# A decoder-layer step: the sample loop runs in four turns of two samples and two prompt heads instead of eight turns of one

## The chip, the cores and the metric

The kernel is one program on one core of a Trainium2 chip. TensorE (PE) multiplies matrices, VectorE (DVE), ScalarE (ACT) and GpSimd (POOL) work on vectors, SyncE (SP) issues transfers. The metric is the device time in microseconds (us), the median of several runs.

## What is computed

One inference step of one layer, in float32, for a prompt of 256 rows and for 8 samples of one row each, each sample with 2048 past rows of K and V in 16 pages. The width is 1024, attention has 8 heads of 64, the depthwise convolution 512 channels and 31 taps, and the feed-forward part 2816 inner channels.

```python
h = rms_norm(x, g_norm1) * (1.0 + sc1) + sh1
q, k, v, glu_a, glu_b, gate_a, gate_c = split(h @ w_in)        # q, k are normed per head
attn = moba_attention(q, k_all, v_all, pos0, slopes) @ w_attn_proj
u = glu_a * sigmoid(glu_b)
cv = depthwise_causal_conv(concat(conv_past, u), w_dwconv) + b_dwconv
cv = silu(layer_norm(cv)) @ w_conv_proj
mix = (sigmoid(gate_a) * attn + sigmoid(gate_c) * cv) @ w_out
x = x + gt1 * mix
h2 = rms_norm(x, g_norm2) * (1.0 + sc2) + sh2
x = x + gt2 * ((silu(f_g) * f_u) @ w_ffn_out)                  # f_g, f_u = halves of h2 @ w_ffn_in
```

`moba_attention` lets each query see its own block of 256 rows and the three past blocks whose mean key fits it best. The outputs are the rows of both groups, their new K and V rows, and the last rows of the convolution's input. sh, sc and gt are parts of `silu(c) @ w_ada + b_ada`.

## The kernel before, in words

All 264 rows (256 prompt, 8 samples) lie transposed, channels on the partitions. Each engine has its own list of instructions in an order written by hand, and semaphores tie the lists together; an engine whose next instruction waits does nothing else meanwhile.

**Prelude.** Modulation, norm, and the columns of q, k, v and the first two pairs of GLU columns (a0, b0, a1, b1). These are made as three products of high and low parts (`split`, L1459).

**The sample loop**, `for b in range(B)`, eight turns. Turn b finishes sample b and prompt head b, and does meanwhile the scoring of sample b + 1 on VectorE. The scoring of one sample is four steps, each a multiplication of four pages of K with the sample's query (`multiply`, L1053, 128x2048) and a reduction over the head's 64 channels (`add_up`, L1060). Both work on one buffer `prod`, so each waits for the one before. K comes in 16 chunks of half a sample by indirect DMA from POOL's queue, into a ring of three places, V in 16 such chunks into a ring of two. The small instructions of a turn lie between these halves:

- the sample: block sums by PE (L1621), their copy (L1156, the first instruction of a turn on VectorE), the gates of the blocks, a ranking of the 8 blocks and penalties (L1168 to L1186), the mask (L1650), maximum (L1198, L1205), exp on ACT, sum (L1220), weights `pg` (L1232); then PE's product with V (`weigh_values`, L1607), the turn of its result (`turn_values`, L1614)
- the head: scores by PE (`prompt_scores`), ALiBi (L1165), maxima (L1170, L1173), exp and scaling on ACT, transposes (L1675), product with V (L1690)
- on PE, to fill gaps, the gate columns g0 to g15 and the rest of the GLU columns (a2, b2, a3, b3), three in a turn (`tile`, L1455); ACT evacuates them with Sigmoid
- on ACT and POOL the 120 taps of the convolution, 20 in each of six turns: a scaled copy (ACT) and an addition (POOL, L575).

The layer norm over the convolution's channels is done in turns 6 and 7. The last turn has no scoring and no gate column.

**After the loop** come the UNITS: eight columns of the convolution's projection (`conv_unit`, cp0 to cp7), eight of attention's (ap0 to ap7), eight of w_out, 44 and then 8 of the feed-forward part (the last in three pieces each). Each unit's weights are split by ACT and VectorE into high and low parts (`whi`, `wlo`), at most four units ahead. Before unit 0, `weigh_values(7)` is issued. Between the units stand the remaining modulations, by ADA_AFTER: modulation(4) behind unit 3, modulation(5) behind unit 9, modulation(6) behind unit 13.

**SyncE** issues the loads of weights one after another in the order of SLOTS, each when its place is free. The order around the change is the gate slots mix0 to mix6, then conv, attn, mod4, out0, mod5, out... as

```python
         + ["conv", "attn", "mod4", "out0", "mod5", "mod6", "out1", "mod7", "mod8", "mod9"]
```

mod5 takes the place of mod4 once modulation(4) has read it. out0 lies in the memory that V's ring had, and for it SyncE has

```python
                if name == "out0":
                    sp.wait_ge(v_used, CH * B)
```

where v_used counts the two halves of each `weigh_values`, 16 in all.

Of the kernel before, what the change touches and what calls it, by code (L numbers as in the profile page):

```python
# [48 lines left out]
THIRD = {0: "a2", 1: "b2", 2: "a3", 3: "b3", 4: "g10", 5: "g13"}  # L49
FIRST_GATE = (0, 2, 4, 6, 8, 11, 14)  # L50


SLOTS = (["ada0", "ada1", "ada2", "ada3", "q", "k", "v", "glu"] + [f"mix{n}" for n in range(B - 1)]
# [17 lines left out]
ADA_AFTER = {3: 4, 9: 5, 13: 6, FIRST_OUT + 1: 7, FIRST_OUT + 3: 8, FIRST_OUT + 5: 9}  # L71
ADT_AFTER = {5: 4, 11: 5, 15: 6, FIRST_OUT + 2: 7, FIRST_OUT + 4: 8, FIRST_OUT + 6: 9, FIRST_FFN + 5: 10, FIRST_FFN + 9: 11}
# [3 lines left out]
PLACE = dict(zip(SLOTS, [0, 1, 2, 0, 1, 2, 0, 1] + [n % 2 for n in range(B - 1)]))  # L76
# [7 lines left out]
         + [f"{x}{t}" for x in "qkv" for t in range(4)] + ["a0", "b0", "vn0", "vn1", "vs", "ks", "kn0", "kn1", "so", "a1", "b1"])  # L84
for _b in range(B - 1):
    FILLS.append(f"g{FIRST_GATE[_b]}")
    if _b == B - 2:
        FILLS += ["ct", "lnm"]
    FILLS.append(f"g{FIRST_GATE[_b] + 1}")
    FILLS.append(THIRD.get(_b, "lnv"))  # L90
# [19 lines left out]
for _b in range(B - 1):  # L110
    LAST_FILL[f"mix{_b}"] = THIRD.get(_b, f"g{FIRST_GATE[_b] + 1}")

# [3 lines left out]
CONV_LOOPS = 6  # L116
CONV_PART = CT * (TAPS - 1) // CONV_LOOPS
CONV_SPLIT = (6, 6, 8)


def program(nc, x_prompt, x_sample, cache_k, cache_v, state_conv, page_table, c_prompt, c_sample,
# [3 lines left out]
    with ExitStack() as ctx:  # L125
# [9 lines left out]
        def sem(name):  # L135
# [20 lines left out]
        inquad = sb("inquad", [P, QU, P], F32R)  # L156
# [11 lines left out]
        sall = sb("sall", [P, 2, PG, H])  # L168
        s1 = sb("s1", [P, PG + 1, H])
        sown = sb("sown", [P, B, H])  # L170
        pg = sb("pg", [P, PG, H])
# [4 lines left out]
        gsT = sb("gsT", [P, QU])  # L176
        gate = sb("gate", [H, NB])
        lanes = pvm[:, 0:P]
        cmp1, cmp2 = (mrow[0:H, 0, 64 * e:64 * e + 64].rearrange("p (m n) -> p m n", m=NB) for e in range(2))
        pen = sb("pen", [H, NB, H], F32R)  # L180
        spots = pvm[:, P:2 * P]
        powns = gs[:, :, 0:H]
        tiny = sb("tiny", [P, 64])
        m1, nmx, dg, es, rinv, pown = (tiny[:, 0:8], tiny[0:H, 8:9], tiny[0:H, 16:24], tiny[:, 24:32],
                                       tiny[:, 32:40], tiny[32:32 + B, 40:48])
        bars = tiny[0:H, 56:64]
        pmx, psum_, prin = tiny[:, 48:50], tiny[:, 50:52], tiny[:, 52:54]
# [40 lines left out]
        vrow = vT[32:32 + B, :, :].rearrange("p t r -> p (t r)")[:, 0:A]  # L228
        snat = u[0:B, 2:4, TAPS - 1:TAPS - 1 + A // 2]
# [12 lines left out]
        soq = s1[0:B, 0:2 * B, :].rearrange("p g h -> p (g h)").rearrange("p (t n) -> p t n", t=2)  # L242
        headsums = oT[0:2 * H, 0, :]
        samples = pg[:, :, :].rearrange("p g h -> p (g h)")
# [22 lines left out]
        modrow_bank, modcol_bank = psS[:, 0:P], chain[:, 0:P]  # L267
        spread_factor = small[:, 0:R]
        normbank = [psS, psT, chain, small, psS, psT]
        sums_, gate_, mask_, turned_ = small[:, 0:QU], small[0:H, 8:8 + NB], small[:, 0:P], small[0:H, P:2 * P]  # L270
        spread_max, spread_sum = small[:, 0:H], small[:, 16:16 + H]
# [44 lines left out]
        ln_c, ln_s, cv_ready = sem("ln_c"), sem("ln_s"), sem("cv_ready")  # L316
# [60 lines left out]
        def conv_part(b, part):  # L377

            if b >= CONV_LOOPS:
                return range(0)  # L380
            first = CONV_PART * b + sum(CONV_SPLIT[:part])
            return range(first, first + CONV_SPLIT[part])


        @block.sync
        def _(sp):
            def load(name):
# [5 lines left out]
                if name == "mod4":  # L393
                    sp.wait_ge(v_full[CH - 1], 16 * B)
# [31 lines left out]
                elif kind == "mix":  # L426
                    wide = P * (3 if THIRD.get(num, "")[:1] == "g" else 2)
                    parts = [(full[:, :, 0:wide], cols(w_in, glu0 + 2 * C + P * FIRST_GATE[num], wide))]
                    if num < 4:
                        parts.append((full[:, :, 2 * P:3 * P], cols(w_in, glu0 + C * (num % 2) + P * (num // 2 + 2), P)))  # L430
# [36 lines left out]
        def _(pool):  # L467
# [57 lines left out]
            step(g.memset(inquad[:, :, :].bitcast(F32), 0.0))  # L525
            for q in range(QU):
                step(g.memset(inquad[0:H, q, 32 * q:32 * q + 32].bitcast(F32), 1.0))
# [40 lines left out]
            def add_taps(b, part):  # L568

                for i in conv_part(b, part):  # L570
                    t = i // (TAPS - 1)
                    pool.wait_ge(prod_ready, i + 1)
                    if i >= 1:
                        pool.wait_ge(conv_added, i)
                    g.tensor_tensor(cvT[:, t, 0:S], cvT[:, t, 0:S], cprod[:, i % CONV_RING, :], ALU.add)\  # L575
                        .then_inc(conv_added, 1)
# [11 lines left out]
            for name in ON_POOL:  # L588
# [3 lines left out]
                if name == "k0":  # L592
                    gather_k(1)
                if name == "v0":
                    pool.wait_ge(acc_full, NUMBER[LAST_FILL["k"]] + 1)
                    gather_k(2)
                if name == "v2":
                    gather_k(3)
                if name == "v3":
                    gather_v(0, 0)  # L600
                if name == "b1":
                    gather_k(4)
            for b in range(B):
# [4 lines left out]
                else:  # L608
                    for c in range(CH):
                        gather_v(b, c)  # L610
# [314 lines left out]
        def _(dve):  # L925
# [210 lines left out]
            for b in range(B):  # L1136
# [86 lines left out]
                if b == 6:  # L1223
                    center()
# [558 lines left out]
```

## Time and profile before

| what | value |
|---|---|
| median of 3 runs | 582.43 us (580.84 to 582.52) |
| the profiled execution's own time | 581.04 us |
| its span, first to last instruction | 579.3 us |
| mean granted TensorE clock | 0.953 of full speed |
| busy: PE, DVE, ACT, POOL | 521.1, 395.7, 292.4, 170.2 us |
| read and written in HBM | 159.1 MB, 275 GB/s over the span |

Busy time is an average over stages with different limits, so the rows below are taken from single stretches. Times in rows are microseconds from the start of the span, unless ns is written. One PE matmul on float32 shows as two instructions, and its end is modelled: where it counts, PE's pace is read from start to start.

### The profile page before, as it was taken

How to read it: one execution, taken by the hardware profiler on the slowest of the kernel's cores; microseconds unless marked ns; L12 is line 12 of the kernel's file. 1: busy time of each engine (PE TensorE's matmuls, PEld its weight loads, DVE VectorE, ACT ScalarE, POOL GpSimd, SP SyncE). 2: the span in 40 equal slices, each digit the busy share in tenths (PEclk: the TensorE clock that was granted, in tenths of full speed). 3: DMA queues.
4: the chain of work that ended last, by engine and by line, in shares of the span. 5: the costliest groups of instructions: out<-in, count | busy, mean ns of one | idle time of the engine just before them, and what ended most of it. 6: DMA issues, size and time to landing. Idle time of an engine off the chain costs nothing.

```text
span 579.3 us, 10395 instructions
## 1 busy us (share of the span) xinstructions
PE 521.1 (90%) x4166; PEld 440.6 (76%) x4166; DVE 395.7 (68%) x609; ACT 292.4 (50%) x519; POOL 170.2 (29%) x232
## 2 busy tenths in 40 slices
PE   3769899888989889798879999599999999999997
PEld 3558688764565557456539999499999999999996
DVE  0643683789999799999766886758565656555441
ACT  3234434587777677755474542383444444433431
POOL 8416378288777586760100000000000000000000
PEclk9589899989989798999969999899999999999999
DMA  8999549698999999999689969937565456476501
GB/s 302 371 359 385 192 164 374 227 351 304 405 411 398 406 345 406 381 402 387 253 328 371 387 244 372 364 129 227 183 216 185 147 176 164 107 200 173 148 18 38
DMA packets 82127, 159.31 MB, mean 275 GB/s; under 512 B 2572, under 2 KB 61112, under 8 KB 76951
## 3 DMA queue, kind: packets, MB, share of 16 engines
q1 hardware_dynamic: 76256, 89.27, 46.1%
q0 software_dynamic: 5120, 67.71, 29.2%
q10 hardware_dynamic: 703, 1.67, 0.8%
q8 instruction: 33, 0.54, 0.4%
q14 instruction: 15, 0.12, 0.1%
HBM read 156.39 MB, written 2.72 MB: 275 GB/s over the span
## 4 chain that ended last, share of the span: by engine, by line
PE 52%; DVE 23%; DMA 12%; issue 5%; ACT 5%; POOL 2%; ACTq 1%; SPq 1%; DVEq 0%; POOLq 0%
PE acc L1583 11%; PE acc L1584 11%; PE acc L1585 11%; DVE prod L1053 7%; DMA wring<-in_w_in 6%; DVE sall L1060 5%; PE acc L1455 4%; DMA wring<-in_w_ffn_in 2%; DVE wlo L1125 2%; PE acc L1468 2%; DMA more<-in_w_ada 2%; PE acc L1470 2%; PE acc L1469 2%; DMA pr<-in_page_table 2%; PE chain L1607 1%
## 5 line engine op out<-in xcount | busy, mean ns | idle before, releaser
L1125 DVE TENSOR_TENSOR wlo<-wring,whi 128x1024 fp32r<-128x1024 f32 (+2 forms) x84 | 92.0, 1097 | 70.9 <-ACT whi L620 69.9
L620 ACT ACTIVATE whi<-wring 128x1024 fp32r<-128x1024 f32 (+2 forms) x84 | 80.0, 958 | 81.3 <-PE acc L1585 74.4
L1583 PE MATMUL acc<-xlo,whi 128*128 128x264 f32 x384 | 110.1, 287 | 0.3 <-DVE hT L1332 0.2
L1584 PE MATMUL acc<-xhi,wlo 128*128 128x264 f32 x384 | 108.9, 284 | 0.0
L1585 PE MATMUL acc<-xhi,whi 128*128 128x264 f32 x384 | 108.8, 283 | 0.0
L575 POOL TENSOR_TENSOR cvT<-cvT,cprod 128x256 f32<-128x256 f32 x120 | 88.0, 733 | 43.9 <-ACT cprod L620 29.0
L1455 PE MATMUL acc<-hT,wring 128*128 128x264 f32 x336 | 94.2, 425 | 4.1 <-DMA wring<-in_w_in 3.7
L1455 PEld LDWEIGHTS acc<-hT,wring 128*128 128x128 f32 x336 | 65.3, 206 | 18.8 <-DMA wring<-in_w_in 4.2
L1583 PEld LDWEIGHTS acc<-xlo,whi 128*128 128x128 f32 x384 | 72.3, 188 | 1.4 <-issue 0.6
L1060 DVE TENSOR_REDUCE sall<-prod 128x32 f32<-128x2048 f32 x32 | 73.0, 2281 | 0.4
L1584 PEld LDWEIGHTS acc<-xhi,wlo 128*128 128x128 f32 x384 | 72.4, 188 | 0.0
L1585 PEld LDWEIGHTS acc<-xhi,whi 128*128 128x128 f32 x384 | 72.0, 188 | 0.0
L620 ACT ACTIVATE cprod<-u,vt 128x256 f32<-128x256 f32 x120 | 53.6, 501 | 13.8 <-POOL cvT L575 12.8
L1584 PE MATMUL acc<-fhi,wlo 128*128 128x264 f32 x208 | 59.2, 284 | 0.0
L1585 PE MATMUL acc<-fhi,whi 128*128 128x264 f32 x208 | 58.9, 283 | 0.0
L1053 DVE TENSOR_TENSOR prod<-kring,qbc 128x2048 f32<-128x2048 f32 x22 | 50.0, 2273 | 1.3 <-PE qbc L1485 0.7
L1583 PE MATMUL acc<-flo,whi 128*128 128x264 f32 x176 | 50.0, 284 | 0.3 <-ACT yn L620 0.3
L620 ACT ACT_TABLE_LOAD x36 | 46.2, 1283 | 2.3 <-PEq L1772 1.7
L586 POOL TENSOR_TENSOR wrest<-wring,phi 128x1024 fp32r<-128x1024 f32 x14 | 33.9, 2428 | 38.2 <-ACT phi L620 38.2
L1585 PEld LDWEIGHTS acc<-fhi,whi 128*128 128x128 f32 x208 | 39.1, 188 | 0.0
L1584 PEld LDWEIGHTS acc<-fhi,wlo 128*128 128x128 f32 x208 | 39.1, 188 | 0.0
L1468 PE MATMUL acc<-hsplit,phi 128*128 128x264 f32 x120 | 36.5, 304 | 0.8 <-POOL wrest L586 0.8
(317 smaller groups left out, 907.9 us busy)
## 6 DMA issues: line engine op xcount, KB each, us to landing
wring<-in_w_ffn_in SPq DMA_DIRECT2D x22, 1024.0 KB, 8.0
wring<-in_w_ada SPq DMA_DIRECT2D x20, 1024.0 KB, 11.4
wring<-in_w_in SPq DMA_DIRECT2D x12, 1024.0 KB, 11.4
wring<-in_w_ffn_out SPq DMA_DIRECT2D x16, 704.0 KB, 5.6
more<-in_w_out SPq DMA_DIRECT2D x4, 1024.0 KB, 12.3
more<-in_w_ada SPq DMA_DIRECT2D x4, 1024.0 KB, 12.5
wring<-in_w_in SPq DMA_DIRECT2D x6, 512.0 KB
wring<-in_w_in SPq DMA_DIRECT2D x4, 768.0 KB
```

Of the source, the lines that this page charges most:

```text
L575: g.tensor_tensor(cvT[:, t, 0:S], cvT[:, t, 0:S], cprod[:, i % CONV_RING, :], ALU.add)\
L586: g.tensor_tensor(low, w, high.bitcast(F32), ALU.subtract).then_inc(rest_by_pool, 1)
L620: return nc.scalar.activation(out, in_, f, **kw)
L1053: v.tensor_tensor(prod[:, :, :], k_place[chunk % K_RING][:, g:g + n, :], qbc[b % 2][:, :].unsqueeze(1).to_broadcast([P, n, A]), ALU.mult). ...
L1060: v.tensor_reduce(sall[:, b % 2, n * half:n * half + n, :].rearrange("p g h -> p (g h)"), prod[:, :, :].rearrange("p g (h d) -> p (g h) d" ...
L1125: v.tensor_tensor(wlo[:, place, 0:n, :], w, whi[:, place, 0:n, :].bitcast(F32), ALU.subtract)\
L1455: ins = mm(bank[:, 0:R], w[:, k, P * t:P * t + P], src[:, k, :], start=k == 0, stop=k == KD - 1)
L1468: mm(bank[:, 0:R], high[:, k, :], hlo[:, k, :], start=k == 0, stop=False)
L1469: mm(bank[:, 0:R], low[:, k, :], hhi[:, k, :], start=False, stop=False)
L1583: mm(bank[:, 0:R], whi[:, place, k - k0, :], lo[:, k, :], start=k == 0, stop=False)
L1584: mm(bank[:, 0:R], wlo[:, place, k - k0, :], hi[:, k, :], start=False, stop=False)
L1585: ins = mm(bank[:, 0:R], whi[:, place, k - k0, :], hi[:, k, :], start=False, stop=k == nk - 1)
```

## The change

The loop becomes four turns of a pair of samples and two prompt heads. What a sample needs between its scores and its weights is done for both at once: block sums, ranking, mask, maxima, exp, sum, weights (128 x 2 x 16 x 8 instead of 128 x 16 x 8). The head's work stays per head. Scoring stays a turn ahead, which is now two samples ahead: sample 1 is scored before the loop too, and each of the first three turns scores two samples, eight steps, of which the last three have nothing between their halves. The fourth turn scores nothing, and holds both samples' and both heads' work, the whole layer norm and the four gate columns g12 to g15. `weigh_values(7)` and `turn_values(7)` move from the start of the units to behind conv unit 5 and 6. modulation(5) moves from behind unit 9 to behind unit 7. The wait of mod4's load for V is dropped, that of out0 stays. Gate and GLU columns have five slots of four columns instead of seven of three. POOL issues some gathers of K and V earlier, and takes the taps in parts of five, 40 in each of three turns.

Sigmoid(x) is written as (1 + tanh(x/2)) / 2: ACT does Tanh with scale 0.5, VectorE adds 1 in the product that follows, and the half goes into GLU's copy and into gt1. The layer norm's root is split in a scaling on VectorE and a Sqrt on ACT.

In the order of VectorE's, ACT's and PE's lists (context lines of the loop on VectorE are the old instructions at their new place):

```diff
+PAIRS = B // 2
+TILES = (("a2", "b2", "a3", "b3", "g0", "g1"), tuple(f"g{n}" for n in range(2, 7)),
+         tuple(f"g{n}" for n in range(7, 12)), tuple(f"g{n}" for n in range(12, 16)))
+MIX = [["a2", "a3", "b2", "b3"]] + [[f"g{4 * n + t}" for t in range(4)] for n in range(4)]
+HOME = {name: (f"mix{n}", t) for n, names in enumerate(MIX) for t, name in enumerate(names)}
...
-ADA_AFTER = {3: 4, 9: 5, 13: 6, FIRST_OUT + 1: 7, FIRST_OUT + 3: 8, FIRST_OUT + 5: 9}
-ADT_AFTER = {5: 4, 11: 5, 15: 6, FIRST_OUT + 2: 7, FIRST_OUT + 4: 8, FIRST_OUT + 6: 9, FIRST_FFN + 5: 10, FIRST_FFN + 9: 11}
+ADA_AFTER = {3: 4, 7: 5, 13: 6, FIRST_OUT + 1: 7, FIRST_OUT + 3: 8, FIRST_OUT + 5: 9}
+ADT_AFTER = {5: 4, 10: 5, 15: 6, FIRST_OUT + 2: 7, FIRST_OUT + 4: 8, FIRST_OUT + 6: 9, FIRST_FFN + 5: 10, FIRST_FFN + 9: 11}
...
-                if name == "mod4":
-                    sp.wait_ge(v_full[CH - 1], 16 * B)
                 if name == "out0":
                     sp.wait_ge(v_used, CH * B)
...
+                if name == "k2":
+                    gather_v(0, 0)
...
+            gather_k(5)
+            pool.wait_ge(acc_full, NUMBER["b1"] + 1)
+            gather_v(0, 1)
+            for i in range(PAIRS):
+                gather_k(4 * i + 6)
+                add_taps(i, 0)
+                if i >= 1:
                     for c in range(CH):
-                        gather_v(b, c)
-                add_taps(b, 1)
-                gather_k(CH * b + 5)
-                add_taps(b, 2)
-                gather_k(CH * b + 6)
+                        gather_v(2 * i, c)
+                add_taps(i, 1)
+                gather_k(4 * i + 7)
+                add_taps(i, 2)
+                add_taps(i, 3)
+                gather_k(4 * i + 8)
+                add_taps(i, 4)
+                for c in range(CH):
+                    gather_v(2 * i + 1, c)
+                add_taps(i, 5)
+                gather_k(4 * i + 9)
...
-                    freed(func(cvT[:, t, :], bank[:, 0:R], ACT.Sigmoid), f"b{t}")
+                    freed(func(cvT[:, t, :], bank[:, 0:R], ACT.Tanh, scale=0.5), f"b{t}")
...
+            last, a = PAIRS - 1, B - 2
+            act.wait_ge(k_used, STEPS * B)
+            for n in range(AHEAD):
+                split_weights(n)
+            head_exp(a)
+            column(last, 0)
+            values_copied(a - 1)
+            tails_of_conv()
+            head_scaled(a)
+            column(last, 1)
+            values_out(a - 1)
+            sample_exp(last)
+            head_turned(a)
+            column(last, 2)
+            head_out(a)
+            head_exp(a + 1)
+            column(last, 3)
+            wait_freed(act, "lnv")
+            func(lnf, lnf, ACT.Sqrt).then_inc(ln_v, 1)
+            head_scaled(a + 1)
+            values_copied(a)
+            values_out(a)
+            head_turned(a + 1)
+            head_out(a + 1)
+            conv_rows()
 
             def split_row(t, ready):
...
-                if n_unit >= 2:
-                    split_weights(n_unit + AHEAD)
+                split_weights(n_unit + AHEAD)
                 if n_unit - 1 in ADA_AFTER:
                     mod_rows(ADA_AFTER[n_unit - 1])
-                if n_unit == 5:
+                if n_unit == 6:
+                    values_copied(B - 1)
+                if n_unit == 7:
+                    values_out(B - 1)
                     act.wait_ge(ownt_ready, 2)
...
+            score(1, 1)
+            score(1, 2)
+            own_scores()
+            dve.wait_ge(consts, 3)
+            gated_glu(0)
+            dve.wait_ge(u_ready, 1)
+            score(1, 3)
...
+                multiply_next(0)
+                turned_sums(i)
                 add_up_next(0)
+                if i == 0:
+                    gated_glu(1)
                     wait_freed(dve, "so")
+                head_scores(a)
+                penalties(i)
                 multiply_next(1)
+                masked(i)
                 add_up_next(1)
+                head_inverse(a)
+                diagonal(i)
                 multiply_next(2)
+                below_maximum(i)
+                if i == 0:
+                    gated_glu(2)
                 add_up_next(2)
+                partition_sums(i)
                 multiply_next(3)
+                weights(i)
                 add_up_next(3)
+                if i == 0:
+                    gated_glu(3)
+                multiply_next(4)
+                head_scores(a + 1)
+                add_up_next(4)
+                head_inverse(a + 1)
+                for n in range(5, 2 * STEPS):
+                    multiply_next(n)
+                    add_up_next(n)
+                if i == 0:
                     dve.wait_ge(stored, 16 * 7)
...
+            last, a = PAIRS - 1, B - 2
+            turned_sums(last)
+            head_scores(a)
+            penalties(last)
+            samples_convolution()
+            masked(last)
+            head_inverse(a)
+            diagonal(last)
+            center()
+            below_maximum(last)
+            split_weights(0)
+            partition_sums(last)
+            weights(last)
+            bank = when_full(dve, "lnv")
+            freed(v.tensor_scalar(lnf, bank[:, 0:R], 1.0 / C, EPS, ALU.mult, ALU.add), "lnv")
+            head_scores(a + 1)
+            split_weights(1)
+            head_inverse(a + 1)
+            split_weights(2)
+            dve.wait_ge(ln_v, 1)
+            step(v.reciprocal(lnf, lnf))
+            scale_rows()
+            for t in range(CT):
+                dve.wait_ge(rhi_ready, t + 1)
+                v.tensor_tensor(clo[:, t, :], cvT[:, t, :], chi[:, t, :].bitcast(F32), ALU.subtract)\
+                    .then_inc(rlo_ready, 1)
+            conv_branch(0)
...
+            for i in range(PAIRS - 1):
+                a = 2 * i
+                first = 1 if i == 0 else 0
+                block_sums(i)
+                column(i, 0, k1=5)
+                gates_of_blocks(i)
+                if i >= 1:
+                    weigh_values(a - 1)
+                else:
+                    column(i, 0, k0=5)
+                    column(i, 1, k1=5)
+                mask(i)
+                column(i, first, k0=5)
+                column(i, first + 1, k1=4)
+                turn_maxima(i)
+                if i >= 1:
+                    turn_values(a - 1)
+                spread_query(a + 3)
+                column(i, first + 1, k0=4)
+                spread_maxima(i)
+                turn_head(a, a)
+                column(i, first + 2)
+                total(i)
+                weigh_head(a)
+                prompt_scores(a + 1)
+                column(i, first + 3, k1=6)
+                weigh_values(a)
+                column(i, first + 3, k0=6)
+                turn_values(a)
+                if i < PAIRS - 2:
+                    spread_query(a + 4)
+                column(i, first + 4, k1=4)
+                turn_head(a + 1, a + 1)
+                column(i, first + 4, k0=4)
+                weigh_head(a + 1)
+                prompt_scores(a + 2)
+            last, a = PAIRS - 1, B - 2
+            block_sums(last)
+            column(last, 0)
+            gates_of_blocks(last)
+            weigh_values(a - 1)
+            to_rows("ct", u, S, TAPS - 1 + B)
+            mask(last)
+            pe.wait_ge(ln_c, 1)
+            sums("lnm", cvT, CT)
+            column(last, 1)
+            turn_maxima(last)
+            turn_values(a - 1)
+            spread_maxima(last)
+            turn_head(a, a)
+            pe.wait_ge(ln_c, 2)
+            sums("lnv", lnsq, CT)
+            column(last, 2)
+            total(last)
+            weigh_head(a)
+            prompt_scores(a + 1)
+            column(last, 3)
+            weigh_values(a)
+            turn_values(a)
+            turn_head(a + 1, a + 1)
+            weigh_head(a + 1)
...
-            weigh_values(B - 1)
-            conv_unit(0)
-            conv_unit(1)
-            turn_values(B - 1)
-            for t in range(2, KD):
+            for t in range(KD):
+                if t == 6:
+                    weigh_values(B - 1)
+                if t == 7:
+                    turn_values(B - 1)
                 conv_unit(t)
                 if t == 4:
                     pe.wait_ge(ownrow_ready, 1)
```

The new functions are the old groups under names: `turned_sums` is L1156, `head_scores` L1165, L1170 and L1173, `head_inverse` L1203, `penalties` L1168 to L1186 without the maxima, `masked` L1195 and L1198, `diagonal` L1205 and L1207, `below_maximum` L1214, `partition_sums` L1220, `weights` L1227 to L1234. On PE `column(i, n)` is the n-th column of TILES[i], in part where k0 or k1 is given; `turn_head` and `weigh_head` are L1675 and L1690. In `penalties` each instruction now waits for the one before it, while before the head's maxima lay between them.

## Rows read from the trace of the kernel before

**Rows 1.** The chain that ended last, shares of the span by engine.

```profile
PE 52%; DVE 23%; DMA 12%; issue 5%; ACT 5%; POOL 2%; ACTq 1%; SPq 1%; DVEq 0%; POOLq 0%
```

**Rows 2.** Busy us (instructions) per engine, PE's clock, DMA share, GB/s.

```profile
157.80:182.70 24.90, 22.32 (x120) 14.54 (x116) 24.08 (x32) 18.91 (x40) 18.44 (x25) 0.93 1.03 404
...
234.90:259.30 24.40, 20.87 (x120) 13.56 (x116) 24.00 (x32) 16.93 (x35) 17.39 (x23) 1.00 1.00 399
...
283.50:302.00 18.50, 14.74 (x96) 6.15 (x97) 11.20 (x31) 10.16 (x24) 1.89 (x2) 0.72 0.65 250
```

**Rows 3.** VectorE's timeline, scoring steps: start, duration, instruction.

```profile
64.00 2.29 DVE L1053 TENSOR_TENSOR prod<-kring,qbc 128x2048 f32<-128x2048 f32 x1 [0.71 <-PE qbc L1485]
...
68.71 2.29 DVE L1053 TENSOR_TENSOR prod<-kring,qbc 128x2048 f32<-128x2048 f32 x1
...
230.25 2.29 DVE L1060 TENSOR_REDUCE sall<-prod 128x32 f32<-128x2048 f32 x1
232.67 2.29 DVE L1053 TENSOR_TENSOR prod<-kring,qbc 128x2048 f32<-128x2048 f32 x1
234.87 0.15 DVE L1156 COPY gsT<-small 128x4 f32<-128x4 f32 x1
...
259.28 0.15 DVE L1156 COPY gsT<-small 128x4 f32<-128x4 f32 x1
```

**Rows 4.** VectorE's timeline, small instructions with POOL adding taps, and after.

```profile
237.19 0.60 DVE L1165 SCALAR_TENSOR_TENSOR pr<-distm,slopes,psS 128x384 f32<-128x384 f32 x1
...
238.50 0.61 DVE L1175 SCALAR_TENSOR_TENSOR mrow<-mrow,lower 8x64 f32<-8x64 f32 x1
...
262.90 0.20 DVE L1175 SCALAR_TENSOR_TENSOR mrow<-mrow,lower 8x64 f32<-8x64 f32 x1
```

**Rows 5.** VectorE's timeline, end of the prelude, and the layer norm's centring.

```profile
96.02 0.48 DVE L1042 SCALAR_TENSOR_TENSOR qkvT<-qkvT,vt,psT 128x264 f32<-128x264 f32 x1
104.82 0.16 DVE L1156 COPY gsT<-small 128x4 f32<-128x4 f32 x1 [8.32 <-PE small L1621]
...
275.17 1.26 DVE L1111 TENSOR_TENSOR cvT<-cvT,cprod 128x1056 f32<-128x1056 f32 x1
```

**Rows 6.** PE's timeline: half a gate column, value products, first and last conv unit's edges.

```profile
246.31 2.05 PE L1455 MATMUL acc<-hT,wring 128*128 128x264 f32 x8
...
257.31 3.62 PE L1607 MATMUL chain<-vring,pg 128*8 128x512 f32 x32
...
283.11 0.38 PE L1621 MATMUL small<-quad,sall 128*128 128x4 f32 x2 [0.80 <-DVE sall L1060]
...
296.63 5.08 PE L1607 MATMUL chain<-vring,pg 128*8 128x512 f32 x32
301.65 0.39 PE L1583 MATMUL acc<-clo,whi 128*128 128x264 f32 x1
...
318.59 0.36 PE L1583 MATMUL acc<-fhi,whi 128*128 128x264 f32 x1 [0.74 <-DVE wlo L1125]
```

**Rows 7.** ACT's timeline: a table load before an exp, and the four Silus.

```profile
263.13 1.28 ACT L620 ACT_TABLE_LOAD   x1
264.42 0.40 ACT L620 ACTIVATE pr<-pr,tiny 128x128 f32<-128x128 f32 x1
...
295.86 2.10 ACT L620 ACTIVATE cvT<-cvT,vt 128x264 f32<-128x264 f32 x4
```

**Rows 8.** SyncE's timeline: the issue of out0, and of mod5 with mod6.

```profile
301.79 0.92 SPq L446 DMA_DIRECT2D more<-in_w_out  x2
310.58 2.66 SPq L446 DMA_DIRECT2D wring<-in_w_ada  x4
```

**Rows 9.** PE's timeline, modulation(5).

```profile
321.67 1.95 PE L1386 MATMUL psS<-wring,cT 128*32 128x128 f32 x64
```

**Rows 10.** The page's DMA issues: size of each, median us from issue to landing.

```profile
wring<-in_w_ffn_in SPq DMA_DIRECT2D x22, 1024.0 KB, 8.0
wring<-in_w_ada SPq DMA_DIRECT2D x20, 1024.0 KB, 11.4
```

More of the change, by code:

```diff
@@ L83 @@
 FILLS = (["c"] + [f"x{t}" for t in range(8)] + ["vec", "st0", "st1", "adt"]
[L84 to L90, printed above, removed]
+         + [f"{x}{t}" for x in "qkv" for t in range(4)] + ["a0", "b0", "vn0", "vn1", "vs", "ks", "kn0", "kn1", "a1", "b1", "so"])
+for _i in range(PAIRS - 1):
+    FILLS += TILES[_i]
+FILLS += ["g12", "ct", "lnm", "g13", "lnv", "g14", "g15"]
 for _u, (_name, _, _, _k0, _) in enumerate(UNITS):
@@ L375, in split_tile, with conv_part @@
                     wrest[:, n, :].rearrange("p (k n) -> p k n", k=KD)[:, :, cols], phi[:, SPLIT[name] % PRE_RING, :, :])
[L377 to L382, printed above, removed]
+        def conv_part(i, part):
+            first = CONV_PART * (CONV_PARTS * i + part)
+            return range(first, first + CONV_PART) if i < PAIRS - 1 else range(0)
         @block.sync
@@ L768, in _, with column, tap_products @@
             act.dma_start(v_sample.rearrange("b o h d -> b (o h d)"), vrow).then_inc(stored, 16)
-            def gate(n):
-                bank = when_full(act, f"g{n}")
-                freed(func(gates[:, n, :], bank[:, 0:R], ACT.Sigmoid), f"g{n}")
-            def tap_products(b, part):
-                for i in conv_part(b, part):
-                    t, n = i // (TAPS - 1), 1 + i % (TAPS - 1)
+            glu("a", 1)
+            glu("b", 1)
+            bank = when_full(act, "so")
+            freed(func(sown[:, :, :].rearrange("p b h -> p (b h)"), bank[:, 0:B * H], ACT.Copy), "so")
+            def column(i, n):
+                if n < len(TILES[i]):
+                    name = TILES[i][n]
+                    if name[0] == "g":
+                        bank = when_full(act, name)
+                        freed(func(gates[:, int(name[1:]), :], bank[:, 0:R], ACT.Tanh, scale=0.5), name)
+                    else:
+                        glu(name[0], int(name[1:]))
+            def tap_products(i, part):
+                for m in conv_part(i, part):
+                    t, n = m // (TAPS - 1), 1 + m % (TAPS - 1)
                     if n == 1:
@@ L1570, in _ @@
             prompt_scores(0)
+            to_rows("kn0", kT, 0, P)
+            to_rows("kn1", kT, P, P)
+            split("a1")
+            split("b1")
+            spread_query(2)
+            pe.wait_ge(so_ready, 1)
+            bank = bank_for("so")
+            mm(bank[:, 0:B * H], ones[0:B, :], soq[:, 1, :], start=True, stop=True).then_inc(acc_full, 1)
             pe.wait_ge(sel_ready, 2)
@@ L1674, in _, with total, turn_head @@
+            def total(i):
+                pe.wait_ge(es_ready, i + 1)
+                mm(spread_sum, ones[:, :], es, start=True, stop=True).then_inc(tot_ready, 1)
+            def turn_head(h, values):
+                pe.wait_ge(pn_ready, 2 * h + 2)
+                pe.wait_ge(po_ready, h)
+                pe.wait_ge(o_ready, 2 * values)
                 for t in range(3):
```

500 lines of the change are left out of this document (220 added, 280 removed).

## The prediction

> **What bounds the kernel now.** I read the chain of waits first, then busy time by stretch, then the timelines of the engines, then the queue of SyncE. Half of the chain is TensorE, a quarter VectorE, an eighth DMA [rows 1]: different stages have different limits. In the sample loop (105 to 283 us) VectorE is busy 24.0 of 24.4 us in a turn, while TensorE, at 20.9, has gaps; DMA moves 399 to 404 GB/s with its engines fully busy [rows 2]. So VectorE sets the loop and DMA is close behind. From 301.65 us TensorE runs almost without a gap [rows 6], and whatever moves the first conv unit, or puts a hole behind it, moves the end.
>
> VectorE's turn, from one block-sum copy (L1156) to the next, takes 259.28 - 234.87 = 24.41 us [rows 3]. Eight halves of scoring cost 2.20 each from start to start (232.67 to 234.87) = 17.6; a multiplication right behind a reduction, with nothing between, costs 2.42, so 0.22 more; the other 6.6 us are small instructions.
>
> **The prelude.** VectorE ends the head norms at 96.4 and then idles 8.32 us until 104.82 [rows 5]. The change scores sample 1 there. add_up(1,0) ends near 98.8. A step with nothing between its halves takes 68.71 - 64.00 = 4.71 us [rows 3], so two steps end at 108.2, own scores and the first GLU at 110.3 (these took 104.90 to 106.9 before), and the third step at 114.9. Sample 2's query and K chunk are there by then by the order of PE and POOL. The loop thus starts at 114.9 instead of 104.8, with one sample more scored: the idle time is gone.
>
> **A turn of two samples.** 16 halves x 2.20 = 35.2 us; seven joints between halves without filler add 1.2 (4.71 against 2 x 2.20 is 0.31 for each two joints, [rows 3]). Two head scores and inverses, which stay per head, cost 2 x 1.25 = 2.5 (the largest, 0.60, is in [rows 4]). The rest of a turn, 6.6 - 1.25 = 5.35, comes once for a pair instead of twice, but six of its instructions become 128 elements longer: at (0.60 - 0.20) us / 320 elements [rows 4] 0.16 each, 1.0 in sum. Together 35.2 + 1.2 + 2.5 + 5.35 + 1.0 = 45.2 against 2 x 24.4. Some of the 5.35 is extra time beside POOL: the same 8x64 instruction takes 0.61 us while POOL adds taps and 0.20 after it has stopped [rows 4]. I keep it, since POOL has as many taps to add.
>
> Three pairs are 135.6, the three GLU products left 1.3: 114.9 + 136.9 = 251.8. Waits: before, most came from ACT's table loads, at 1.28 us one [rows 7], some five in a turn. The loads go (below). I take 1.8 us of waits; the bounds are 0.6 (a turn of before without any) and 8. Scoring ends at 253.6, 29.5 us before the 283.1 of now [rows 6]. TensorE is no bound here: five gate columns at 2 x 1.9, two value products at 3.6 [rows 6] and some 8 us of small work are 34 us of 45.
>
> **Tanh for sigmoid.** In the trace each change between gate and exp has a load of 1.28 us, and the next activation starts 0.01 us after it [rows 7]. Whether tanh shares exp's tables no row shows, since before has no tanh: with shared tables some ten loads in a pair go, 12.8 us of ACT; with separate ones none. I take shared, and price the other as a rival. ACT is off VectorE's path but for waits, so either way the sum moves by those alone. The Trainium skill (ScalarE: Activation LUTs, "Table sets: the hidden batching unit") lists tanh in exp's set and in sigmoid's too. Its "What ACT_TABLE_LOAD costs" gives 2.66 us for a switch, drain included, which would make the ten loads 26.6 us; the row shows no drain. The added half and plus one ride in instructions that exist already, and cost nothing that this trace can show.
>
> **The tail.** This is what pays for it. Before, from the last reduction (283.06) to conv_unit(0) at 301.65 are 18.6 us, and weigh_values(7) is already done in them [rows 6]. Now the last turn carries two samples' weights, two heads, the layer norm's mean, centring and variance, and four gate columns, in one order on PE. From scoring's end: PE had nothing for about 9 us, so it starts at the lower level, 1.2 GHz (the same value product takes 5.08 us in this stretch, whose granted clock is 0.72 in the mean, and 3.62 in the loop [rows 2, 6]). Block sums and g12, which stand before the gates, to 6.6; gates and value product of sample 5 to 10.3; conv rows, mask, mean sums (1.9) to 13.4; g13 to 17.2; maxima, values turned, spread to 18.6; VectorE centres (1.26 twice and 0.4, [rows 5]) to 20.8; variance sums 22.7; g14 26.5; total, weigh_head(6), scores(7) 28.3; g15 32.1; values of sample 6 35.5; then a chain with nothing beside it, copy 0.6, turn 0.9, out 0.4, turn_head 0.4, copy 0.5, weigh_head 1.0, out 0.4, to 40.0; table load 1.28, four Silus 2.1, first high part and its rest 0.8 (load and Silu: [rows 7]): conv_unit(0) at 44.5. Bounds: 41.5 if PE has full clock all through, 48 if it has half for twice as long.
>
> So conv_unit(0) starts at 253.6 + 44.5 = 298.1, 3.5 us earlier. But weigh_values(7) now lies behind it, before unit 6: + 3.5 (at 3.62 less the overlap), and PE's 4 to 5 idle us before unit 0 leave it at half clock: + 1.5. Sum so far: + 1.5.
>
> **The new wait.** The order of SP's queue is conv, attn, mod4, out0, mod5. out0 still waits for v_used = 16, that is for weigh_values(7), and everything behind it waits too. Today that is met at 301.7, so out0 is out of the way when mod5 becomes free (mod4 read, issue at 310.58; out0 went at 301.79 [rows 8]), and modulation(5), after unit 9 at 321.67, finds its data: landed within 11.1 us [rows 8, 9]. After the change, count from conv_unit(0): eight units take 318.59 - 0.74 - 301.65 = 16.2 with modulation(4) 1.95, own values 1.0 and turned values 0.9 in them [rows 6, 9], so a unit is 1.54. Six units, modulation(4) and own values: 12.2. weigh_values(7) ends at 15.7; only now SP issues out0 (0.92 [rows 8]), and mod5 at 16.6. PE needs two units and the turn, 4.0, and asks for mod5 at 19.7, since its modulation is moved from behind unit 9 to behind unit 7. The 2 MB land 11.4 us after issue by the median of w_ada [rows 10]: 28.0. Stall 8.3, taken as 9 with the slow clock behind it. Bounds: 5 (8 us to land, as w_ffn_in [rows 10]) and 12. Everything on PE behind it, ap0 first, waits. Later loads wait for PE's progress and shift along.
>
> The Trainium skill (DMA: Bandwidth & Descriptors, "Queues, rings and completion order") says that each DMA engine consumes a queue's descriptors in ring order. By it mod5's 2 MB would stand behind out0's 2 MB rather than beside them: the stall would be the upper bound's 12 and the time 594.5 instead of 591.5. No row of this trace separates the two; both lie in the forecast.
>
> Sum: - 3.5 + 3.5 + 1.5 + 9 = + 10.5 us on the profiled 581.04: 591.5, and as the median of the runs is 1.4 above that, I say 592.
>
> **Rivals.** (1) *mod5 is in time*: the load is fast, or PE comes later, and hides it. For it: before, no modulation of this stage waited. Against: issue and use were then 11.1 us apart [rows 8, 9], now 3.1. It gives 581.04 + 1.5 = 582.5, no change, and decides alone: for each us that the stall shrinks, one comes back. With the tail at full clock too (- 4) it is faster, 578.5. (2) *DMA becomes the loop's bound.* A pair needs eight chunks of 2.1 MB (K and V) and 1.25 slots of gate weights, 19 MB; at 404 GB/s [rows 2] 47 us against VectorE's 45.2, at a tenth less 52. The lead in K (three chunks) covers the first pair. 3 to 15 us more: 595 to 606. (3) *PE's clock*: the tail stays at full clock, -3 to -4.5: 587.5. (4) *The loads stay*, if tanh has other tables than exp: a load of 1.28 stands before sample_exp again, and before the exps of both heads; one of them shows per pair, two in the tail's last chain: 5 us more, 597.
>
> **Numbers.** Forecast (loop shorter by 29, tail longer by 26, stall of 5 to 12): 0.58, 587 to 597, (3) in it; (2) and (4), slower still: 0.15; (1) without change: 0.11; (1) with a shorter tail or loop, faster: 0.16. A measurement here tells 0.3% from no change (580.7 to 584.2). Range to hold eight in ten: 578 to 601; the likeliest case's own is 587 to 597. Faster 0.16, same 0.11, slower 0.73.
>
> **What would show it.** Right: VectorE without gap from 96 to about 254; no table load between gates and exps; scoring's end to first conv unit over 40 us; PE idle 5 to 12 us behind conv unit 7 for wring<-in_w_ada, the longest single wait of that stage. Wrong: that wait is absent; or scoring ends after 262 with multiplications waiting for K; or the tail is under 38.

## The result: 595.6 us, slower by 2.3%

| | before | after |
|---|---|---|
| median | 582.47 us (580.84 to 584.45) | 595.59 us (594.34 to 595.88) |
| ratio after to before | | 1.0227, 95% interval 1.0191 to 1.0263 |
| span of the profiled execution | 579.3 us | 594.0 us |
| mean granted TensorE clock | 0.953 | 0.925 |
| busy: PE, DVE, ACT, POOL | 521.1, 395.7, 292.4, 170.2 us | 517.0, 385.6, 255.8, 169.5 us |

Some executions, of whatever kernel, are slower as a whole; the medians here and below take in all of them, the ratios leave these out, so the two can differ.

Every engine is busy for less time than before, and the kernel is slower. So no engine was given more work; the difference lies in what waits for what, and in what a wait brings with it. The page of the kernel after, the chain that ended last by engine and by line:

```profile
PE 54%; DVE 25%; DMA 10%; issue 4%; ACT 4%; SPq 1%; POOL 1%; ACTq 0%; DVEq 0%
PE acc L1697 11%; PE acc L1698 11%; PE acc L1699 11%; DVE sall L1118 9%; DVE prod L1111 8%; PE acc L1561 6%; DMA wring<-in_w_ada 5%; PE chain L1721 2%; DMA wring<-in_w_ffn_in 2%; DMA more<-in_w_ada 2%; PE acc L1574 2%; PE psS L1492 2%; PE acc L1576 2%; PE acc L1575 2%; DVE wlo L1185 1%
```

The modulation weights in `wring` now hold 5% of the chain, where they were not among its fifteen largest lines before. Go through the stages in order of time.

**The loop.** VectorE's timeline after. The copy of the block sums (L1199) comes once for a pair, behind the first multiplication of the next pair; the reductions L1118 are the second halves of scoring steps:

```profile
97.53 2.28 DVE L1118 TENSOR_REDUCE sall<-prod 128x32 f32<-128x2048 f32 x1
...
118.10 0.16 DVE L1199 COPY gsT<-small 128x8 f32<-128x8 f32 x1
...
164.53 0.16 DVE L1199 COPY gsT<-small 128x8 f32<-128x8 f32 x1
...
210.60 0.16 DVE L1199 COPY gsT<-small 128x8 f32<-128x8 f32 x1
...
251.28 2.29 DVE L1118 TENSOR_REDUCE sall<-prod 128x32 f32<-128x2048 f32 x1
254.68 0.17 DVE L1199 COPY gsT<-small 128x8 f32<-128x8 f32 x1 [1.11 <-PE small L1742]
```

The idle 8.3 us of the prelude [rows 5] are gone. A pair takes 46.4, 46.1 and, up to the last copy with its wait of 1.1, 44.1 us. The last reduction ends at 253.57; before, it ended at 283.06 [rows 6]. Busy time by stretch, one line for each turn of the loop:

```profile
118.10:164.50 46.40, 37.91 (x178) 26.36 (x177) 45.48 (x46) 26.41 (x67) 34.96 (x47) 0.87 0.98 393
164.50:209.60 45.10, 36.45 (x201) 24.10 (x200) 43.01 (x43) 26.91 (x68) 35.60 (x47) 0.88 0.96 391
209.60:253.60 44.00, 34.85 (x197) 23.01 (x196) 43.03 (x42) 25.11 (x65) 33.93 (x46) 0.93 0.99 399
```

VectorE (third number) still sets the loop; DMA is at 0.96 to 0.99 of its engines, nearly a second bound.

**The tail of the loop.** TensorE's timeline: the four gate columns (L1561), the two value products (L1721) and conv_unit(0), at 299.05:

```profile
253.62 1.02 PE L1742 MATMUL small<-quad,sall 128*128 128x4 f32 x4 [7.78 <-DVE sall L1118]
254.50 6.53 PE L1561 MATMUL acc<-hT,wring 128*128 128x264 f32 x16
...
267.78 3.72 PE L1561 MATMUL acc<-hT,wring 128*128 128x264 f32 x16
...
277.05 3.72 PE L1561 MATMUL acc<-hT,wring 128*128 128x264 f32 x16
...
282.66 3.80 PE L1561 MATMUL acc<-hT,wring 128*128 128x264 f32 x16
286.39 3.62 PE L1721 MATMUL chain<-vring,qkvT 128*8 128x512 f32 x32
...
299.05 0.56 PE L1697 MATMUL acc<-clo,whi 128*128 128x264 f32 x1 [4.75 <-DVE clo L1347]
```

From the end of scoring to conv_unit(0) are now 45.5 us, where there were 18.6. TensorE has 27.43 busy us in the first 29.5 of them, VectorE 11.36. The bound changed hands: before the copy it was VectorE, behind it TensorE, with work that used to lie under VectorE's scoring. So 29.5 us of earlier scoring have become 2.6 us of earlier conv_unit(0) (299.05 for 301.65 [rows 6]).

**Behind it.** SyncE's queue after, and modulation(5) on TensorE:

```profile
286.49 0.92 SPq L442 DMA_DIRECT2D wring<-in_w_ada  x2
317.42 0.92 SPq L442 DMA_DIRECT2D more<-in_w_out  x2
318.38 6.16 SPq L442 DMA_DIRECT2D wring<-in_w_ada  x4
```

```profile
313.74 3.62 PE L1721 MATMUL chain<-vring,qkvT 128*8 128x512 f32 x32
318.84 0.95 PE L1729 MATMUL psT<-headof,pvm 128*128 128x2 f32 x8
330.75 3.64 PE L1492 MATMUL psS<-wring,cT 128*32 128x128 f32 x64 [9.39 <-DMA wring<-in_w_ada]
```

out0's load goes only when weigh_values(7) is done (317.42; before, 301.79 [rows 8]), mod5's stands right behind it, and TensorE waits 9.39 us for it. Busy time by stretch shows what SyncE's wait does to the transfers (DMA share and GB/s are the last two numbers, TensorE's clock the one before them):

```profile
299.00:304.00 5.00, 4.95 (x22) 4.98 (x23) 2.74 (x6) 1.53 (x4) 0.00 (x0) 0.50 0.83 355
304.00:318.00 14.00, 14.00 (x163) 10.55 (x161) 6.55 (x14) 4.03 (x7) 0.00 (x0) 0.99 0.01 2
```

```profile
321.00:335.00 14.00, 4.61 (x70) 3.80 (x70) 2.58 (x7) 1.68 (x5) 0.00 (x0) 0.64 1.05 390
```

For 14 us nothing is transferred, though TensorE is fully busy, and then TensorE stands still while everything is transferred at once. In the kernel before, DMA moved 371 GB/s from 304 to 318 us.

### The profile page after: what moved, and what is told of

It reads as the page before. It is cut to its first block, busy times and chain, and to the rows that moved or that the text cites. A ratio compares the mean times of both kernels' runs of the same rounds, so it can differ in the third digit from the quotient of the medians.

```text
span 594.0 us, 10187 instructions
## 1 busy us (share of the span) xinstructions
PE 517.0 (87%) x4110; PEld 442.5 (74%) x4110; DVE 385.6 (65%) x539; ACT 255.8 (43%) x486; POOL 169.5 (29%) x229
## 4 chain that ended last, share of the span: by engine, by line
PE 54%; DVE 25%; DMA 10%; issue 4%; ACT 4%; SPq 1%; POOL 1%; ACTq 0%; DVEq 0%
PE acc L1697 11%; PE acc L1698 11%; PE acc L1699 11%; DVE sall L1118 9%; DVE prod L1111 8%; PE acc L1561 6%; DMA wring<-in_w_ada 5%; PE chain L1721 2%; DMA wring<-in_w_ffn_in 2%; DMA more<-in_w_ada 2%; PE acc L1574 2%; PE psS L1492 2%; PE acc L1576 2%; PE acc L1575 2%; DVE wlo L1185 1%
## 5 line engine op out<-in xcount | busy, mean ns | idle before, releaser
L1561 PE MATMUL acc<-hT,wring 128*128 128x264 f32 x336 | 93.3, 433 | 2.1 <-DVE hT L1071 2.0
L1561 PEld LDWEIGHTS acc<-hT,wring 128*128 128x128 f32 x336 | 69.4, 213 | 20.3 <-issue 5.3
L1118 DVE TENSOR_REDUCE sall<-prod 128x32 f32<-128x2048 f32 x32 | 73.1, 2283 | 0.6
L624 ACT ACTIVATE cprod<-u,vt 128x256 f32<-128x256 f32 x120 | 55.2, 501 | 19.7 <-POOL cvT L570 19.2
L1574 PE MATMUL acc<-hsplit,phi 128*128 128x264 f32 x120 | 36.7, 306 | 1.2 <-POOL wrest L581 0.8
L1576 PE MATMUL acc<-hsplit,phi 128*128 128x264 f32 x120 | 35.0, 292 | 0.0
```

The costliest lines, as they stand in the source:

```text
L624: return nc.scalar.activation(out, in_, f, **kw)
L1118: v.tensor_reduce(sall[:, b // 2 % 2, b % 2, n * half:n * half + n, :].rearrange("p g h -> p (g h)"), prod[:, :, :].rearrange("p g (h d) - ...
L1561: ins = mm(bank[:, 0:R], w[:, k, P * t:P * t + P], src[:, k, :], start=k == 0, stop=k == KD - 1)
L1574: mm(bank[:, 0:R], high[:, k, :], hlo[:, k, :], start=k == 0, stop=False)
L1576: ins = mm(bank[:, 0:R], high[:, k, :], hhi[:, k, :], start=False, stop=k == KD - 1)
```

## The experiments

Times are medians; each ratio is to the kernel before in the same session, whose median was 580.6 (first four), 582.1 (no gate column behind the scoring) and 582.7 us (the last three).

**1. mod5's load ahead of out0's.** One change in the order of SyncE's loads:

```diff
-         + ["conv", "attn", "mod4", "out0", "mod5", "mod6", "out1", "mod7", "mod8", "mod9"]
+         + ["conv", "attn", "mod4", "mod5", "out0", "mod6", "out1", "mod7", "mod8", "mod9"]
```

> The changed kernel with one edit: in the list of loads mod5 stands before out0. Theory (mod5 is held up in SyncE's queue behind out0's wait for weigh_values(7)): mod5 is issued when modulation(4) has read mod4, near 309.5, and lands at 321 to 323, where TensorE asks for it at 321.4. The wait of 9.4 us shrinks to 0 to 2, and modulation(5) runs at full clock (1.7 us less): 584 to 587 us against 595.6. Rival (the loss lies in the longer tail, or in weigh_values(7) behind it): at most 2 us less, 593 or more. Rival (the wait only moves on, to out0, mod6 or fin0): half comes back, about 590.

Measured: 585.21 us, ratio 1.0091 (1.0062 to 1.0120), span 581.8. That is the theory's number; both rivals fall. TensorE's timeline shows modulation(5) without a wait, and the longest waits of that stage (299 to 420 us) now are others:

```profile
320.21 1.95 PE L1492 MATMUL psS<-wring,cT 128*32 128x128 f32 x64
```

```profile
PE acc L1697 <- DVE clo L1347: 4.8, 1, 4.8
PE psS L1492 <- DMA more<-in_w_ada: 4.7, 1, 4.7
```

The span falls by 12.2 us: 9.39 of wait, 1.7 because the matmuls of modulation(5) no longer run at half clock (3.64 to 1.95), and 1.0 because this execution's conv_unit(0) came at 298.06 by itself. The wait for `more<-in_w_ada` was 2.6 in the change, so a little of the gain is lost again there. The wait behind out0 is shown as the main cause: with it gone, 12.2 of the 14.7 us in the span are back, and the ratio falls from 1.0227 to 1.0091.

**2. Only the use of mod5 moved back** to where it was before, behind unit 9, the loads as in the change:

```diff
-ADA_AFTER = {3: 4, 7: 5, 13: 6, ...
-ADT_AFTER = {5: 4, 10: 5, 15: 6, ...
+ADA_AFTER = {3: 4, 9: 5, 13: 6, ...
+ADT_AFTER = {5: 4, 11: 5, 15: 6, ...
```

> The changed kernel with one edit: modulation(5) and its transpose back behind units 9 and 11, where they were before. The load still goes out behind weigh_values(7), at 318.4. Theory: TensorE asks for mod5 two units, 2.9 us, later, so the wait of 9.4 becomes 6.5 and nothing else changes: 592.7 us. Rival (the place of modulation(5) is the cause and the queue is not): the wait is gone, 584 to 586. Rival (the load takes up whatever time it is given, since the queues are shared): no change, 595.6.

Measured: 593.33 us, ratio 1.0183 (1.0114 to 1.0253), span 591.2. The wait is 5.3 us for 9.4 (6.5 were expected), as two units lie ahead of it now. So the earlier use costs some 3 us of the stall (2.8 in the span); the late issue is the rest.

**3. weigh_values(7) ahead of unit 0,** turn_values(7) ahead of unit 2, ACT's copies at the same places. That frees out0's load early, with SyncE's order unchanged:

```diff
-                if t == 6:
+                if t == 0:
                     weigh_values(B - 1)
-                if t == 7:
+                if t == 2:
                     turn_values(B - 1)
```

> The changed kernel with one edit: weigh_values(7) again before conv unit 0, turn_values(7) after unit 1, and ACT's copies with them. Theory: V's last two chunks are only issued when weigh_values(6) has read its halves (287 and 290) and land at 302 to 304, so TensorE idles before conv unit 0 instead, which starts near 308 at the lower clock. out0 is then out of the way, mod5 goes out after modulation(4) at about 316 and lands at 328, wait 3 to 5 us. Sum: 591 to 594 us, little better than 595.6. Rival (moving weigh_values(7) behind unit 5 is the loss, and taking it back returns it): 584 to 586.

Measured: 590.11 us (587.38 to 592.81), ratio 1.0159 (1.0079 to 1.0240), span 585.6: a us below the theory's range, and the rival of 584 to 586 fell. The profile is of an execution of 587.53 us, at the lower end of the four. TensorE's longest waits from 293 to 420 us:

```profile
PE chain L1722 <- DMA vring<-in_cache_v,rowof: 6.7, 2, 5.5
PE chain L1864 <- DVE gates L1408: 3.6, 1, 3.6
PE psS L1493 <- DMA more<-in_w_ada: 2.0, 1, 2.0
PE psS L1493 <- DMA wring<-in_w_ada: 1.7, 1, 1.7
```

The wait for mod5 shrinks to 1.7, and a wait for sample 7's V takes its place: behind a scoring that ends early, V has not landed yet, and conv_unit(0) starts only at 306.15. Where weigh_values(7) was put in the change hides that, and its own 3.6 us are work that must be done on one side of conv_unit(0) or the other.

**4. tanh alone,** on the kernel before.

```diff
-freed(func(gates[:, n, :], bank[:, 0:R], ACT.Sigmoid), f"g{n}")
+freed(func(gates[:, n, :], bank[:, 0:R], ACT.Tanh, scale=0.5), f"g{n}")
```

(and with it the plus one and the halves, as in the change.)

> The kernel before with only the sigmoids through tanh (copies with the half, plus one in VectorE's products, gt1 halved). Theory (exp and tanh share their tables, ACT is off VectorE's path but for waits): some 29 table loads of 1.28 us go, and of VectorE's waits for ACT in the loop, 4.8 us in sum, 3 to 4 us: 578.5 to 579.5 against 582.5. Rival (the loads carry more, since TensorE's transposes wait for ACT's scaled scores): 572 to 576. Rival (tanh sits in other tables, the loads stay): 582 or more.

Measured: 582.78 us (577.16 to 600.88), ratio 1.0001 (0.9950 to 1.0051), span 578.3. Loads of tables fall from 36 to 8, and no gain can be told. In its profile the loop is shorter by 3.7 us, but two waits take part of that: VectorE's in the prelude is 9.43 for 8.32 [rows 5], and one of 2.13 on a TensorE result is new. The theory had 3 to 4 us of gain; the interval leaves room for 2.9 at most. So the number of loads came as expected and the time did not: a miss of the theory's price.

**5. Sigmoid again, with mod5's load first.** As in 1, with all tanh edits undone.

> The changed kernel with modulation(5)'s weights ahead of out0's in SP's order and with Sigmoid in place of Tanh everywhere (the halvings taken out with it). It prices the table loads in the new order of work: about 36 loads of 1.28 us instead of 7. Theory (the loads sit in gaps of ACT, whose busy share of the loop is 88.0 of 156.7 us, and DVE sets the loop's end): the scoring ends within 1.5 us of the 253.7 of the kernel that differs only in this, and the total is 585 to 587. Rival (each load delays the sums and exps that DVE waits for, as my fourth rival had it): 5 us more, 589 to 591, with waits of DVE on ACT in the loop. Rival from the kernel before with tanh alone: no difference at all, 584.5 to 586.

Measured: 585.32 us (582.98 to 588.90), ratio 1.0067 (1.0037 to 1.0097), where 1 has 1.0091 (1.0062 to 1.0120). No difference; the 5 us more of the first rival would be a ratio of 1.018. ACT's table loads with Tanh (the change; 1 has the same seven), then in this kernel:

```profile
L624 ACT ACT_TABLE_LOAD x7 | 9.0, 1283 | 1.8 <-PEq L1927 1.7
```

```profile
L624 ACT ACT_TABLE_LOAD x31 | 39.8, 1283 | 2.3 <-PEq L1926 1.7
```

Some 31 us of ACT's time are saved and nothing comes of it. The profiled execution was the slowest of this kernel's twelve (588.90): its scoring ends 5 us later, but 3.0 of these stand there at the first copy of the block sums already (120.25 for 117.25), so this pair of executions prices the loads in the loop at 2 us at most.

**6. No gate column behind the scoring.** As in 1, with the columns of the four turns set to 6, 7, 7 and 0:

```diff
-TILES = (("a2", "b2", "a3", "b3", "g0", "g1"), tuple(f"g{n}" for n in range(2, 7)),
-         tuple(f"g{n}" for n in range(7, 12)), tuple(f"g{n}" for n in range(12, 16)))
+TILES = (("a2", "b2", "a3", "b3", "g0", "g1"), tuple(f"g{n}" for n in range(2, 9)),
+         tuple(f"g{n}" for n in range(9, 16)), ())
...
                 weigh_head(a + 1)
                 prompt_scores(a + 2)
+                column(i, first + 5)
+                column(i, first + 6)
```

> The changed kernel with mod5 loaded before out0 (as in the run before) and g12 to g15 taken out of the last turn: turns 1 and 2 do seven columns each, the last two of each where TensorE idled about 8 us before the block sums. Theory (TensorE's order of work is the bound of the tail, 33 us of 45, four columns of 3.8 us in it): conv unit 0 starts 31 us after the last reduction instead of 45, the chain of the last head and the layer norm then being the bound; 1 to 2 us are given back before the last block sums. 585 - 14 + 1.5 = 572 to 574 us. Rival (the chain over ACT and VectorE, with V's last chunks, bounds the tail): 581 to 585. Rival (the gate weights land late in the loop, DMA being near its bound): scoring ends 3 to 6 us later, 575 to 579.

Measured: 582.53 us (574.86 to 587.98), ratio 0.9977 (0.9934 to 1.0020), span 580.1. A miss: 572 to 574 us were expected, 11 to 13 below kernel 1. The medians are 2.7 us apart, the spans 1.7, the ratios 1.1%. Scoring's end to conv_unit(0) did shrink as expected, from 45.5 (298.06 less 252.6 in kernel 1) to 34.5 us (297.18 less 262.69). But scoring ended 10 us later. TensorE's timeline, g12 in the third pair:

```profile
228.74 0.59 PE L1602 MATMUL psS<-qkvT 64*128 64x256 f32 x2
238.59 4.87 PE L1563 MATMUL acc<-hT,wring 128*128 128x264 f32 x12 [9.26 <-DMA wring<-in_w_in]
```

The weights of g12 were not there earlier: they share DMA engines that are busy 0.99 of the time in that turn of the change with K and V. Behind that column in TensorE's order stands weigh_values(4), behind this in ACT's order the copy of its result and the exps of the next head, and VectorE waited 9.95 us for these exps. So the third rival had the mechanism, at 10 us instead of its 3 to 6.

**7. Two columns behind the scoring.** As in 1, with 6, 6, 6 and 2 columns. g12 stands where its weights were seen to land; g14 and g15 fill TensorE's waits around weigh_values(6):

```diff
-TILES = (("a2", "b2", "a3", "b3", "g0", "g1"), tuple(f"g{n}" for n in range(2, 7)),
-         tuple(f"g{n}" for n in range(7, 12)), tuple(f"g{n}" for n in range(12, 16)))
+TILES = (("a2", "b2", "a3", "b3", "g0", "g1"), tuple(f"g{n}" for n in range(2, 8)),
+         tuple(f"g{n}" for n in range(8, 14)), tuple(f"g{n}" for n in range(14, 16)))
...
+            column(last, 0)
             weigh_values(a)
+            column(last, 1)
             turn_values(a)
```

> The changed kernel with modulation(5)'s weights ahead of out0's, and the gate columns of the four turns set to 6, 6, 6 and 2 instead of 6, 5, 5 and 4: g12 and g13 go into the third turn, at its end, where their weights have landed; g14 stands before weigh_values(6) and g15 behind it, where PE waited for the cache's V and for ACT's copy. Theory (PE's order sets the tail, and the four columns are 6.5 us at half the clock and 3 x 3.5 of it; without all four the tail was 34.5 us): the scoring ends at 253.5 to 254.5, conv_unit(0) starts 37 to 40 us behind it, at 291 to 293.5, the span is 574 to 578 and the time 577 to 581, below the kernel before. Rival (the weights of g12 still arrive too late and hold the scoring, or modulation(4)'s and (5)'s weights are waited for in place of what is saved): span 579 to 582, time 582 to 585.

Measured: 576.35 us (575.35 to 577.35), ratio 0.9902 (0.9864 to 0.9940), span 575.3: 1.0% faster than the kernel before, faster than the change, and just below the 577 to 581 that the theory had. The wait for g12's weights is 0.58 us, the scoring ends where it did, and conv_unit(0) starts at 290.70:

```profile
238.80 2.05 PE L1560 MATMUL acc<-hT,wring 128*128 128x264 f32 x8 [0.58 <-DMA wring<-in_w_in]
...
253.44 1.02 PE L1741 MATMUL small<-quad,sall 128*128 128x4 f32 x4 [4.21 <-DVE sall L1117]
...
290.70 0.56 PE L1696 MATMUL acc<-clo,whi 128*128 128x264 f32 x1 [4.76 <-DVE clo L1346]
```

**8. The same, and ACT does the convolution's rows early,** behind the scaling of the last head's exps:

```diff
+            conv_rows()
             values_copied(a)
...
             head_out(a + 1)
-            conv_rows()
```

> As the kernel with two columns in the tail, and ACT does the Silus of the convolution's rows and their rounded copies right behind the exps of sample 7 instead of behind the last head's output, so that conv_unit(0) does not wait for them behind that head. Theory (the wait of 4.75 us for clo is ACT's order alone: table load, four Silus, four copies): the wait for clo falls below 1 us, and as weigh_values(6)'s copy comes 2 to 3 us later, 2 us are left, a span 1.5 to 2.5 us below that of the other kernel. Rival: the copy of the value products holds the last head's turn as long as it saves; no difference.

Measured: 576.32 us (571.13 to 577.21), ratio 0.9881 (0.9831 to 0.9931), which can't be told from 7. The rival was right. The wait for clo is gone, but the value products' copy comes later and TensorE waits there:

```profile
285.05 1.05 PE L1728 MATMUL psT<-headof,pvm 128*128 128x2 f32 x8 [1.90 <-ACT pvm L624]
...
288.71 0.59 PE L1696 MATMUL acc<-clo,whi 128*128 128x264 f32 x1
```

From the last copy L1198 to conv_unit(0) are 36.5 us (252.17 to 288.71) against 36.2 in 7 (254.50 to 290.70). The span is 1.8 us less only because the whole execution was 2.3 us ahead at that copy.

## Why the prediction came true, step by step

Predicted 592 (587 to 597 for the likeliest case), measured 595.6, with the forecast's sign and near the upper end. The likeliest case's mechanism is the one that came: the tail eats what the loop saves, and the load behind out0 makes the loss. The rival of the other sign fell: mod5 was not in time. One slip is in the last step of the sum: 591.5 and the 1.4 to the median are 592.9, not 592.

- *The loop.* Predicted end of scoring 253.6, measured 253.57. The agreement to the tenth is luck, as two errors of a microsecond cancel: the prelude was 1 us longer, the three pairs with their waits 1 us shorter. VectorE's idle time has no wait longer than 0.8 us in it.
- *The second rival, DMA as the loop's bound,* did not come, but was near: 391 to 399 GB/s at 0.96 to 0.99 of the engines' time. Experiment 6 ran into it.
- *Tanh.* The tables are shared: loads fell from 36 to 7 (to 31 where Sigmoid stays in the new order). The fourth rival priced the loads at 5 us, 0.9%; experiments 4 and 5 show no effect within about 0.5%.
- *The tail.* Predicted 44.5 us, measured 45.5; the worked-out order on TensorE holds to within 1 us at every step (g13's end 17.2 and 17.8, g15's 32.1 and 32.8, the last head's out 40.0 and 40.7). The third rival (full clock in the tail) fell: g12 took 6.53 us for 3.72. Experiments 6 and 7 show that the columns were what set the tail: with none 34.5, with two in TensorE's waits 37.3 (290.70 less 253.4).
- *Slow clock in front of unit 0.* Predicted 1.5, measured 2.4: the first eight groups of three matmuls come 0.66 us apart at a granted clock of 0.50, the next ones 0.365:

```profile
299.84 0.42 PE L1697 MATMUL acc<-clo,whi 128*128 128x264 f32 x1
300.50 0.42 PE L1697 MATMUL acc<-clo,whi 128*128 128x264 f32 x1
...
304.80 0.28 PE L1697 MATMUL acc<-clo,whi 128*128 128x264 f32 x1
305.17 0.28 PE L1697 MATMUL acc<-clo,whi 128*128 128x264 f32 x1
```

- *weigh_values(7) behind unit 0.* Predicted 3.5, measured 3.62.
- *The wait for mod5.* Predicted 9, of which 8.3 are the wait and 0.7 the slow clock behind it; measured 9.39 and 1.7 for the modulation at half clock, 11.1 in all.

The sum of the measured terms is - 2.6 + 3.6 + 2.4 + 9.4 + 1.7 = + 14.5 us, against + 14.7 in the span; the prediction had + 10.5. What was mis-sized is the clock (2.4 and 1.7, where 1.5 and 0.7 stood), 1.1 of the wait (9.4 for 8.3), 0.9 us of conv_unit(0)'s start and 0.1 of weigh_values(7). Each is a term of the right sign. The sum leaves out that the old wait of 0.74 us in front of unit 8 [rows 6] is gone; with it the terms give 13.8, and TensorE is 14.04 us late at modulation(6) (343.73 for 329.69). The last 0.7 us arise behind it and were not traced.

Whether mod5 moved behind out0 or beside it can be read from the landings. Each load is two halves of 1 MB. out0's, issued at 317.42 and 317.83, landed 5.2 and 7.5 us later, the second at 325.3. mod5 was complete at 330.7. mod6's halves, issued at 319.9 and 322.0, landed 13.5 and 14.2 us later, the second at 336.2. So the loads came one after the other, some 5.4 us for each 2.1 MB (390 GB/s), and not side by side. This agrees with the rule of the Trainium skill (DMA: Bandwidth & Descriptors, "Queues, rings and completion order") that each DMA engine consumes a queue's descriptors in ring order; no experiment tested it by itself. The stall of 12 that was worked out from it in the prediction was still too high: mod5 was asked for 3.9 us behind out0's issue, as reckoned (4.0), but landed 12.3 us behind its own, where that stall wanted 15. out0, with no load ahead of it, was complete 7.9 us behind its first issue; so the median of 11.4 [rows 10] probably holds some queueing already, and that stall counts out0's transfer on top of it.

## What to carry to other kernels

When the work of two turns is joined, the last turn has no turn behind it to hide under: count what the other engine has to do after the last scoring, not just what the bound engine saves. Here 29.5 us saved on VectorE left 2.6 at the first unit behind the loop. When an instruction that frees a buffer is moved, look in the queue of loads for what stands behind the load that waits for it: standing one entry behind it cost 11 us here, and swapping two names in the order gave them back. And work can be moved out from behind the last turn only as early as its weights can land when DMA is already full: here the loop's 0.96 to 0.99 of the DMA engines' time was the sign that experiment 6 would run into.

## What the runs showed of the hardware

- TensorE's granted clock was 0.50 (1.2 GHz) in the 5 us behind a wait of 4.75, and 0.64 in the mean of the stretch with the wait of 9.39: the waits cost 2.4 and 1.7 us more than themselves, in matmuls at half pace.
- ACT's table loads, 24 fewer at 1.28 us each in kernel 1 than in 5, made no difference to the time that ten and twelve runs could tell (1.0091 and 1.0067); ACT was busy 88 of 156 us in the loop.
- SyncE's wait emptied the DMA engines wholly: 2 GB/s for 14 us between stretches of 355 and 390.
- Three loads of 2.1 MB in SyncE's queue, issued within 5 us, were complete at 325.3, 330.7 and 336.2: one after the other, at 390 GB/s.
